# Where one slot's weights come from during the linear-attention heads: output weights loaded and scaled first, three modulation blocks through another slot, first sums two groups later

## The reference, cut to what matters

```
mod = silu(cond) @ ada_w[l] + ada_b[l]          # six vectors of 1024: shift, scale, gate, twice
h = rmsnorm(x, norm_mix_g[l]) * (1 + sc_m) + sh_m
x = x + g_m * mixer(h)                          # even layer: GLA heads + Fourier groups -> w_out
h = rmsnorm(x, norm_ffn_g[l]) * (1 + sc_f) + sh_f
x = x + g_f * (square(relu(h @ ffn_w1[l])) @ ffn_w2[l])
```

## Time and profile before

| | |
|---|---|
| time, median of 3 runs | 1104.89 us (1104.58 to 1105.58) |
| profiled execution, its own time | 1108.39 us |
| its span, slowest core (core 3) | 1107.3 us |
| spans of the cores | 1105.5, 1104.5, 1106.9, 1107.3, 1102.7, 1100.5, 1100.5, 1101.0 us |
| busy share of the span | PE 96%, DVE 55%, ACT 39%, POOL 15% |
| heads' pipeline | from 94 to about 245 us of the span |

### The profile page before, as it was taken

The page is one execution under the profiler, slowest core; times in us unless marked ns, Lnnn a source line. Parts: engine busy times, 40 slices in busy tenths (PEclk is TensorE's granted clock), DMA queues, the critical chain, the costliest instruction groups (busy, mean ns, idle before and its releaser), DMA issues.

```text
span 1107.3 us, 15395 instructions; the slowest of 8 cores (1100.5 to 1107.3 us)
## 1 busy us (share of the span) xinstructions
PE 1065.3 (96%) x6012; PEld 534.3 (48%) x6012; DVE 611.7 (55%) x1118; ACT 428.8 (39%) x825; POOL 165.2 (15%) x203
## 2 busy tenths in 40 slices
PE   3699999899999999999999999999999999999997
PEld 0356877654444444444444444444444444444445
DVE  5343899966667686878224638567572222222228
ACT  5266899756743000233105611347632001332023
POOL 5001443324100000000104100044000000000021
PEclk9999999999999999999999999999999999999999
DMA  9998872429626856754921221442342142142106
GB/s 220 178 197 131 140 157 52 128 77 204 110 48 105 132 96 104 125 84 70 152 48 29 39 46 31 76 76 49 67 76 48 29 76 48 29 76 48 29 1 228
DMA packets 17737, 101.32 MB, mean 91 GB/s; under 512 B 1898, under 2 KB 7178, under 8 KB 11136
## 3 DMA queue, kind: packets, MB, share of 16 engines
q0 software_dynamic: 9584, 81.07, 42.9%
q1 hardware_dynamic: 7536, 18.87, 5.3%
q10 hardware_dynamic: 544, 0.39, 0.1%
HBM read 166.98 MB, written 7.86 MB: 158 GB/s over the span
## 4 chain that ended last, share of the span: by engine, by line
PE 89%; DVE 4%; DMA 3%; ACT 2%; POOL 1%; issue 1%; ACTq 0%; DVEq 0%; POOLq 0%
PE psf L324 89%; DMA sb_slot<-adaP 3%; DVE sb_X L345 2%; ACT sb_A L339 1%; POOL sb_X L115 0%; PE psf L1175 0%; POOL sb_slot L115 0%; DVE sb_A L345 0%; DVE sb_B L345 0%; DVE sb_A L342 0%; ACT sb_B L339 0%; DVE sb_att L342 0%; ACT sb_X L353 0%; DVE sb_X L342 0%; PE psf L1307 0%
## 5 line engine op out<-in xcount | busy, mean ns | idle before, releaser
L324 PE MATMUL psf<-sb_hT,sb_slot 128*128 128x512 bf16 x2472 | 551.9, 382 | 0.0
L324 PEld LDWEIGHTS psf<-sb_hT,sb_slot 128*128 128x128 bf16 x2472 | 241.3, 98 | 286.7 <-issue 16.2
L324 PE MATMUL psf<-sb_A,sb_slot 128*128 128x512 bf16 (+2 forms) x1696 | 359.5, 371 | 0.0
L324 PEld LDWEIGHTS psf<-sb_A,sb_slot 128*128 128x128 bf16 x1696 | 165.1, 98 | 188.1 <-issue 1.2
L339 ACT ACTIVATE sb_relu<-psf 128x512 bf16<-128x512 f32 x192 | 114.1, 595 | 354.3 <-PE psf L324 353.1
L345 DVE SCALAR_TENSOR_TENSOR sb_X<-psf,sb_modT,sb_X 128x512 f32<-128x512 f32 (+2 forms) x148 | 108.4, 734 | 217.1 <-PE psf L324 216.9
L342 DVE TENSOR_TENSOR sb_A<-sb_relu 128x512 bf16<-128x512 bf16 x192 | 81.5, 425 | 141.4 <-ACT sb_relu L339 141.0
L339 ACT ACTIVATE sb_B<-sb_X 128x512 bf16<-128x512 f32 (+2 forms) x96 | 55.7, 607 | 163.2 <-DVE sb_X L345 145.8
L324 PE MATMUL psf<-sb_slot,sb_hT 128*128 128x192 bf16 (+1 forms) x576 | 79.7, 290 | 0.6 <-ACT sb_X L353 0.2
L566 POOL TENSOR_TENSOR sb_B<-sb_B 128x512 f32<-128x512 bf16 (+2 forms) x48 | 59.3, 1242 | 121.2 <-ACT sb_B L339 120.6
L781 DVE SCALAR_TENSOR_TENSOR sb_B<-sb_slot,sb_B 128x1024 bf16<-128x1024 bf16 x56 | 68.3, 1219 | 0.4
(11 more groups left out here) (143 smaller groups left out, 691.0 us busy)
## 6 DMA issues: line engine op xcount, KB each, us to landing
sb_slot<-w POOLq DMA_DIRECT2D x16, 2048.0 KB, 16.2
sb_slot<-adaw POOLq DMA_DIRECT2D x14, 1024.0 KB, 10.8
sb_slot<-adaw POOLq DMA_DIRECT2D x3, 2048.0 KB, 20.2
sb_X<-xT SPq DMA_DIRECT2D x6, 1024.0 KB, 10.3
sb_X<-xT POOLq DMA_DIRECT2D x8, 512.0 KB, 11.2
sb_slot<-adaP POOLq DMA_DIRECT2D x8, 512.0 KB, 29.5
yT<-sb_X SPq DMA_DIRECT2D x8, 512.0 KB, 2.9
sb_X<-xT POOLq DMA_DIRECT2D x2, 1024.0 KB, 48.0
```

Of the source, the lines that this page charges most:

```text
L324: T.op("pe", lambda: nc.tensor.matmul(out, l, r, start=start, stop=stop), reads=R, writes=W, sig=stop if sig is None else sig)
```

## The change

Three edits:

1. `evO` takes the place of the first ada block in slot 0, straight after the first `adaP` pieces, and stays there until its projection is over. Its six scalings move from iterations 16 to 21 to iterations 0 to 5.
2. The three ada blocks of layer 0 are loaded through slot 1, one after the other, after `evH01` and ahead of `dft`. Their `ada_block` calls move from iterations 1, 6 and 11 to iterations 13, 16 and 19.
3. In both output projections the sums of squares of token block 2, and the start of its norm, are held back by 7 groups of matmuls instead of 5.

```diff
         wadd("evH01", 2 * 8 * 448, evH_d[0])
-        wada(0, 2)
+        wadd("evO", 8192, evO_d)
         wadd("evH23", 2 * 8 * 448 + 1024, evH_d[1])
-        wada(0, 3)
+        for b in range(2, 5):
+            wada(0, b)
         wadd("dft", 8192, dft_d)
-        wada(0, 4)
-        wadd("evO", 8192, evO_d)
-        early = (1, 0, 2, 0, 1, 0, 0)
+        early = (1, 0, 2, 1, 1, 1, 1)
...
+                lag = {MO[0]: 7, MO[1]: 5, MO[2]: 3}[m]
...
-                stat4(m, oc, 3 if m == MO[2] else 5)
+                stat4(m, oc, lag)
...
-                    pe_defer(3 if m == MO[2] else 5, lambda: norm_end(m, nxt))
+                    pe_defer(lag, lambda: norm_end(m, nxt))
...
-            if 16 <= it < 22:
-                evO_scale(it - 16)
+            if it < 6:
+                evO_scale(it)
...
-            if it in (1, 6, 11):
-                ada_block(0, 2 + it // 5)
+            if it in (13, 16, 19):
+                ada_block(0, it // 3 - 2)
```

## The result

The changed kernel takes 1115.0 us, the median of six runs (1114.56 to 1115.85); the kernel before took 1105.47 beside it (six runs, 1104.58 to 1106.31). The ratio is 1.0089, interval 1.0078 to 1.0099: slower by 9.5 us, where +9.1 was forecast. The profiled execution took 1114.83 us, its span is 1113.8, and its slowest core is core 5. Before, the slowest was core 3. In some executions, of several kernels here (five of the six of e5 among them), the cores of a die run at a clearly lower granted clock and take longer; the ratios leave these out.

The account below looks back on a forecast made before the run. PE was taken as the bound, with DVE binding from 173 to 187 us. Terms +11.5 - 2.0 + 0.4 - 0.8 gave +9.1 us, so 1114.0 us against the 1104.89 median; 8-in-10 range 1108.5 to 1119.5.

Parts of the forecast that it names:

- to the start of iteration 20: Heads' pipeline: three chained ada loads make PE wait, so iteration 20 starts 11.5 us late.
- comes back afterwards: From 190.9 to 224 us: PE's 2.9 us of waits, mostly for DVE, shrink by 2.0 us (0 to 2.9).
- clock behind block 4: After PE's wait for ada block 4, some matmuls run at half speed: +0.4 us (0 to +1.3).
- later sums and the rest: First sum of the output projection: PE's 1.03 us wait for POOL's quad goes, -0.8 us (-1.03 to 0).
- The three loads: Slot 1, ada blocks 2, 3, 4: loads of 16.2, 17.3 and 16.2 us; PE waits 7.5, 3.0 and 2.6 us.
- the scalings: Six DVE scalings moved to iterations 0 to 5: priced at 0 there (0 to +0.5 us).
- One sign of being wrong: Span's end: wrong if the waits are there but it does not move by about their sum less 6.
- No change: Rival: ada loads of 13.5 us, so waits and what comes back are equal; chance 0.05.
- Faster: Rival: loads land in time and blocks fill PE's waits in iterations 13 to 19; -3.6 us, 1101.3 us; chance 0.04.
- Much later: Rival: ada loads of 18.5 us put the kernel +15.8 us, at 1120.7 us; chance 0.12.

Follow-up runs that it names:

- e5: The changed kernel run again, unaltered: no ratio, median of six 1132.77 us; its one comparable run took 1112.66 us beside 1103.41 before.
- e1: The changed kernel with each of the three ada loads cut to a quarter of its block: 1104.73 us, ratio 0.9953 to the kernel before.
- e2: The changed kernel with its three ada blocks at iterations 15, 19 and 23 instead of 13, 16 and 19: 1107.36 us, ratio 0.9979 to the kernel before.
- e3: The kernel before with only the third edit, in the even layer's projection (sums and norm 7 groups behind): 1108.12 us, ratio 0.9988.
- e4: The kernel before without the six scalings of the output weights (output lacks that factor): 1107.6 us, ratio 0.9988.
- e6: The changed kernel with 34, 8 and 12 unused matmuls ahead of ada blocks 2, 3 and 4: 1113.92 us, ratio 1.0097 to the kernel before.
- e7: The changed kernel with ada block 2 back at iteration 1, `evO` after it, blocks 3 and 4 at iterations 16 and 20: 1100.72 us, ratio 0.9978 to the kernel before.

## Why the prediction was right, and where only its sum was

The mechanism was right. The loads that follow each other through one slot are the bound of the stage: with short loads the loss turns into a gain (e1), with more room the waits for them vanish (e2). The total was met to 0.4 us, but not by terms that are each right, and that it was met so closely is luck. On core 5, whose terms add up to its +13.3 us:

| term | forecast, us | core 5, us | read from |
|---|---|---|---|
| to the start of iteration 20 | +11.5 | +12.1 | timelines |
| comes back afterwards | -2.0 | -0.5 | iteration 20 |
| clock behind block 4 | +0.4 | +1.7 | 6.67 against 5.00 |
| later sums and the rest | -0.8 | -1.3 | from iteration 21 on; e3 |
| start of iteration 0 | 0 | +1.3 | timelines |

**The three loads.** They were put at 16.2, 17.3 and 16.2 us and took 16.2, 17.5 and 15.6. The first wait is 7.46 (7.5 forecast), the third 2.45 (2.6). The second is 1.19 where 3.0 stood: block 3 landed at 166.24 + 17.5 = 183.7, near the 182.4 forecast, but PE came later, since iteration 14 started 1.1 us later than forecast and ran slowly behind the long wait. The prediction had said that this loss is covered by the next load's wait, and it is; it should also have made that wait smaller by the 2.2 us that iteration 14 took too long. For the sum it makes no difference: the start of iteration 20 follows from the loads alone.

**What comes back: the mis-sized term.** I took -2.0 from waits that I blamed on DVE's lag. e4 takes the scalings out and e1 takes the long waits out, and the same wait of 0.89 us stands there in both; the one for ACT is 0.63 in e4, as before, and 0.86 in e1 and in the changed kernel. From iteration 21 to the Fourier matmuls nothing came back in sum; in iteration 20 a wait of 0.25 and some smaller time did, 5.47 - 5.00 = 0.5 us. The prediction had named the reason itself (the way of one result from engine to engine) and gave it 0.9 of the 2.9 us; it was nearly all.

**The clock: too small.** On core 5 the iteration behind block 4 took 1.7 us too long, above the +1.3 at which the bound stood, because more than six matmuls ran slowly. e6 shows that the idle time is the cause. The Trainium skill ("TensorE: Matmul & The Clock Gate", Part 1) has idle time bring the lower clock; the prediction let it count for a third, and e6 agrees with the page. The page's rule asks for a longer idle stretch than some that did it here: the clock fell behind block 4 after 2.45 us of waiting on core 5 and after 0.59 on core 3. So that all of the +1.3 would be paid did not follow from the page; the rows show it. On the other cores the picture is mixed: iteration 20 took 6.67, 6.67 and 6.40 us on cores 3, 5 and 7 and 5.0 on the rest, whereas iteration 14 took 6.26 to 7.85 on all eight.

**The later sums.** e3 alone brings 1.3 us, and the part of the span behind the heads is 1.3 shorter on core 5. The die with the higher granted clock says the same: from the first Fourier matmul to the end cores 0 to 3 took 880.0 to 880.2 us in e3 and 881.4 to 881.7 in e4, which has the sums as before. The wait was 1.03; nothing else came late.

**Which core is the slowest.** Core 5 lost 13.3 us, the medians only 9.5. There are two reasons in the traces. First, in the profile before, the two dies were not alike: from the first Fourier matmul to the end cores 4 to 7 took 881.4 to 881.8 us and cores 0 to 3 took 885.0 to 887.4, at a lower granted clock (1106.2 us and 0.994 against 1100.7 and 0.998 as medians of the dies); after the change all eight took 879.9 to 880.4. The clock records show where this comes from. Cores 2 and 3 have six stretches of 4 to 7 us at a granted clock of 0.81, 33.3 us in all, cores 0 and 1 have four, 20.9 us, and cores 4 to 7 have none. I estimate 33.3 x 0.19 = 6.2 us and 3.9 us from this, against 5.9 and 3.6 measured. The first of them, on core 3, and the same window on core 5:

```profile
259.00:265.00 6.00, 6.00 (x25) 2.46 (x24) 4.37 (x7) 3.82 (x7) 2.31 (x2) 0.81 1.05 195
...
259.00:265.00 6.00, 6.00 (x29) 2.74 (x28) 5.16 (x8) 4.13 (x7) 3.46 (x3) 1.00 0.96 156
```

No core of the changed kernel's profile has such a stretch. The kernels e1, e3 and e4 have them on cores 4 to 7 and not on 0 to 3. What sets them off isn't shown. So on core 3, which went only from 1107.3 to 1109.6 us, about 5.6 us of the change's cost were hidden by stretches that fell away. How many of the six runs of the kernel before had them can't be read, since these runs have no trace. Second, the loads are not the same on all cores, as told below. The slowest core of the kernel after is one with long loads. The numbers that I took from core 3, 16.2 and 17.3, fit such a core, while core 3 itself had loads of 14.9, 14.6 and 13.7 this time, and lost little. I had not asked how loads differ between cores, beyond core 1's 15.4.

So I count the forecast's mechanism, its place, its three waits (one of them mis-sized) and the scalings as right. On core 5 its terms fell short by 4.2 us in sum: 1.5 for what comes back, 1.3 for the clock, 1.3 for the start of iteration 0 and 0.6 for the loads, less 0.5 for the rest. The total came out because the slowest core before was another one, held up by its clock.

One sign of being wrong was mis-stated: that the span would not move by about the sum of the waits less 6. The forecast's own sum takes 4.0 off 13.1. On core 5 waits of 11.1 us came with a span 13.3 longer, so read by the letter this sign would call the mechanism wrong; e1 and e2 show that it was not.

**The rivals.** "No change" wanted 13.5 us per load. Cores 1, 3 and 6 did have loads near that size (13.0 to 14.9), and even they waited 5.0 to 6.1 us for the first one; what counts is the core with 15.6 to 17.5. The estimate of 13.7 us worked out from the Trainium skill ("DMA: Bandwidth & Descriptors", "Anatomy of one DMA") is near what those cores show and not the others. "Faster" asked for loads that have landed in time; e1 shows its size. "Much later" wanted 18.5 us and no row has that.

## What to carry to other kernels

When loads are chained through one buffer, add up their times from issue to landing and compare with the compute between two uses; here 15.6 to 17.5 us stood against 8.7 for the first and 14 to 15 for the others, and four iterations for each removed the waits. Take the landing time of the slower core of a pair, not the median of one core. Before comparing slowest cores, look at the granted clock of each die: a few short stretches at 0.81 were worth as much as the effect sought. And before letting small waits "come back", ask whether they are lag or the plain way of a result between engines: a wait that has the same 0.89 us in every version is not lag.

## What the runs showed of the hardware

**Two neighbouring cores have loads of unequal length.** In the changed kernel's trace, POOL's issue of the first `adaw` load on cores 4 and 5, each counted from the start of its own span:

```profile
146.91 0.61 POOL L115 DMA_DIRECT2D sb_slot<-adaw  x1 [0.45 <-PE psf L324]
...
147.73 0.61 POOL L115 DMA_DIRECT2D sb_slot<-adaw  x1 [0.45 <-PE psf L324]
```

The second load, which took 17.5 us on core 5, took this on core 4:

```profile
sb_slot<-adaw POOLq DMA_DIRECT2D x1, 2048.0 KB, 15.1
```

In each of the pairs 0/1, 2/3, 4/5 and 6/7 the core whose issue stands earlier has the shorter loads: first load 14.1 against 16.2, 14.9 against 16.8, 14.6 against 16.2, 13.7 against 15.7. The same holds for the second load, and for the first load of a pair in the traces of e2, e5, e6 and e7, 20 pairs of 20, though it is now the even and now the odd core that leads. The lead at the issue was 0.2 to 2.8 us. With quarter loads (e1) it holds in three pairs of four. The spans show what it comes to: in the six runs of the changed kernel the two cores of a pair lie 2.6 to 8.4 us apart (24 pairs, mean 5.6), in the runs of the kernel before 0.1 to 3.0 (152 pairs, mean 1.3 to 1.4), with quarter loads 0.8 and in e7 1.0 on average. Whether the lead is the cause isn't shown. No kernel set it on purpose, and no trace shows that two cores start at the same moment. A rival is open: one core of a pair may be ahead in the whole execution and be early at iteration 11 for that reason. In the changed kernel the `evH23` load at 91 to 94 us already has the same order (14.4 us on core 1 against 16.9 on core 0).

**Small transfers beside a large one.** The initial states (96 KB, SP) took 13.0 us beside block 3's load on core 5, and 3.7 us beside `dft`. `dft` itself (2048 KB, SP) took 7.4 us there, where it was the only large one (7.4 to 9.6 on the eight cores), and on core 3 of the kernel before 14.9 beside `evO` (10.6 to 18.1). A quarter of an ada block took 5.0 us on core 5 (4.9 to 6.6 on the eight cores), not a quarter of 16.

**The clock falls after short waits, but not always.** Block 4 followed a wait of 0.59 us on core 3, and iteration 20 took 6.67 us; on core 2 it followed one of 0.65, and iteration 20 took 5.01. What separates the two isn't shown. Where no wait stood in front of a block (e1, e2, e7), its 64 matmuls of two columns did not bring the clock down.
